# Mixers' out-projection: six of eight products as three fp32r products of split parts, the first of them moved into the recurrence's last chunk

## The reference, cut to what matters

```python
# per layer (twice); h is the normed, modulated input, 256 x 1024
o_att  = sliding_window_sink_attention(...)   # 512 features: 4 blocks of 128
o_rwkv = recurrence, group norm, bonus, gate  # 256 features: 2 blocks
o_conv = short gated convolution              # 256 features: 2 blocks
x = x + gate * (concat(o_att, o_rwkv, o_conv) @ w_mix_out)   # 1024 x 1024
x = x + gate2 * swiglu(norm(x))
```

## Time and profile before

| | before |
|---|---|
| median of 3 runs | 1794.88 us (1794.59 to 1794.94) |
| the profiled execution's own time | 1799.44 us |
| its span, first to last instruction | 1797.6 us |
| mean granted TensorE clock | 0.992 of full |
| layer 0: last output-projection product ends | 1052.84 us |
| layer 1: the same | 1601.94 us |

### The profile page before, as it was taken

How to read it: one execution, slowest core, us unless ns; L and a number is a source line. 1 busy time by engine, 2 the same in 40 slices (tenths; PEclk the granted TensorE clock), 3 DMA queues, 4 the chain that set the end, 5 groups by cost and what they waited for, 6 DMA issues and landing times.

```text
span 1797.6 us, 31559 instructions
## 1 busy us (share of the span) xinstructions
PE 1758.6 (98%) x13254; PEld 1604.7 (89%) x13254; DVE 1204.9 (67%) x1757; ACT 809.5 (45%) x1075; POOL 19.4 (1%) x25
## 2 busy tenths in 40 slices
PE   9999999999999999999999999999999999899999
PEld 8889879788887788999997799999999997789999
DVE  3895456777887877887637468777877456546443
ACT  2326443534576765434435254344443435335342
POOL 0000000000000000000000000000000000000000
PEclk9999999999999999999999899999999999999999
DMA  8434420787898986787441057876677432034442
GB/s 322 141 118 164 161 74 1 299 332 296 324 359 336 359 335 262 298 336 294 185 164 49 25 222 311 332 298 266 255 306 305 188 128 85 25 141 188 170 182 71
DMA packets 65228, 391.33 MB, mean 218 GB/s; under 512 B 7360, under 2 KB 7488, under 8 KB 27328
## 3 DMA queue, kind: packets, MB, share of 16 engines
q1 hardware_dynamic: 64800, 389.25, 56.0%
q10 hardware_dynamic: 288, 0.08, 0.0%
HBM read 388.25 MB, written 1.05 MB: 217 GB/s over the span
## 4 chain that ended last, share of the span: by engine, by line
PE 86%; DVE 8%; ACT 3%; issue 1%; DMA 1%; POOL 0%; SPq 0%; DVEq 0%; ACTq 0%
PE bank L526 85%; DVE region L2248 1%; PE bank L567 1%; DVE slab_low L1929 1%; ACT region L1432 1%; DMA slab<-in_w_up 0%; DVE region L1976 0%; DMA region<-in_w_down 0%; DVE tiny L1978 0%; DVE region L1987 0%; DVE region L2211 0%; DVE d_low L1936 0%; DVE tiny L2210 0%; DVE xT L2041 0%; DMA xT<-in_x 0%
## 5 line engine op out<-in xcount | busy, mean ns | idle before, releaser
L1929 DVE TENSOR_TENSOR slab_low<-slab,w_hi 128x2048 fp32r<-128x2048 f32 x152 | 346.5, 2292 | 94.3 <-ACT w_hi L1473 93.9
L526 PE MATMUL bank<-h_hi,w_hi 128*128 128x256 f32 x1408 | 391.7, 281 | 0.0
L526 PE MATMUL bank<-h_hi,slab_low 128*128 128x256 f32 x1408 | 390.9, 281 | 0.0
L526 PE MATMUL bank<-h_lo,w_hi 128*128 128x256 f32 x1408 | 380.2, 281 | 0.0
L1473 ACT ACTIVATE w_hi<-slab 128x2048 fp32r<-128x2048 f32 x152 | 291.1, 1917 | 86.9 <-DMA slab<-in_w_ffn_in 66.0
L526 PEld LDWEIGHTS bank<-h_hi,slab_low 128*128 128x128 f32 x1408 | 269.5, 191 | 0.0
L526 PEld LDWEIGHTS bank<-h_hi,w_hi 128*128 128x128 f32 x1408 | 264.7, 188 | 0.5
L526 PEld LDWEIGHTS bank<-h_lo,w_hi 128*128 128x128 f32 x1408 | 257.6, 188 | 0.0
L526 PE MATMUL bank<-gT_hi,d_hi 128*128 128x256 f32 x832 | 234.0, 281 | 0.8 <-DVE gT_lo L2126 0.8
L526 PE MATMUL bank<-gT_lo,d_hi 128*128 128x256 f32 x832 | 233.7, 281 | 0.0
L526 PE MATMUL bank<-gT_hi,d_low 128*128 128x256 f32 x832 | 233.6, 281 | 0.0
(11 more groups left out here) (282 smaller groups left out, 2856.2 us busy)
## 6 DMA issues: line engine op xcount, KB each, us to landing
slab<-in_w_ffn_in SPq DMA_DIRECT2D x88, 1024.0 KB, 8.4
slab<-in_w_up SPq DMA_DIRECT2D x64, 1024.0 KB, 8.7
region<-in_w_ada SPq DMA_DIRECT2D x128, 512.0 KB, 6.5
region<-in_w_ffn_out SPq DMA_DIRECT2D x44, 1024.0 KB, 4.8
region<-in_w_down SPq DMA_DIRECT2D x32, 1024.0 KB, 5.7
slab<-in_w_in SPq DMA_DIRECT2D x23, 1024.0 KB, 4.9
slab<-in_w_mix_in SPq DMA_DIRECT2D x20, 1024.0 KB, 8.2
hT<-in_w_ada SPq DMA_DIRECT2D x16, 512.0 KB, 7.6
```

The costliest lines, as they stand in the source:

```text
L526: return nc.tensor.matmul(o, lhsT, rhs, start=start, stop=True, skip_group_check=True)
L1929: V_.tensor_tensor(slab_low[slot][:, :], slab[slot][:, :], w_hi[h % 3][:, :].bitcast(F), ALU.subtract)\
```

## The change

The weights and the operands of j = 0 to 3 and 6, 7 are split; j = 4, 5 (the recurrence's part) stay plain. ACT makes the high part of out-slab c4 in chunk c4, in two pieces (1024 and 512 columns per partition), and of attention block c4 at the end of the chunk; DVE makes the low parts of slab c4 - 1 and attention block c4 - 1 at the start of chunk c4. The last attention block, the convolution and the last slab follow after the chunks. In chunk 3 TensorE does the products of j = 0 to 2 of block 0 ahead of its wait for `u_ready`, and those of block 1 ahead of the last attention output. The squares of the centred output move from `sq` to `V["kk"]`. In layer 0 SP's loads of w_ada (`ada_loads`, segment 2) now wait for the last out-slab to be used.

```diff
@@ the products (TensorE)
+                    def out_part(b, js):
+                        if b == len(places):
+                            if b % 2 == 0:
+                                out_slab()
+                            places.append(product("dve"))
+                        hi, lo, whole = slabs[b // 2]
+                        cols, ps = slice((b % 2) * P, (b % 2 + 1) * P), places[b][:, 0:T]
+                        for j in js:
+                            if j in (4, 5):
+                                m = mm(ps, whole[:, j, cols], V["yr"][:, j - 4, :])
+                                continue
+                            x_hi, x_lo = (o_hi[:, j, :], o_lo[:, j, :]) if j < 4 else \
+                                (cy_hi[:, j - 6, :], cy_lo[:, j - 6, :])
+                            mm(ps, hi[:, j if j < 4 else j - 2, cols], x_hi, j == 0)
+                            mm(ps, hi[:, j if j < 4 else j - 2, cols], x_lo)
+                            m = mm(ps, lo[:, j, cols], x_hi)
+                        return m
@@ in the chunks
                         outputs("vt", "C2T")
+                        if c4 == 3:
+                            pe.wait_ge(S["o_low"], w("o_low", 3))
+                            out_part(0, range(3))
                         pe.wait_ge(S["u_ready"], w("u_ready"))
...
                         m.then_inc(S["y_done" if c4 == 3 else "y_part"], 1)
+                        if c4 == 3:
+                            out_part(1, range(3))
@@ after the chunks
-                    pe.wait_ge(S["swa_ready"], w("swa_ready"))
-                    pe.wait_ge(S["conv_ready"], w("conv_ready"))
-                    out_early(0)
+                    pe.wait_ge(S["o_low"], w("o_low"))
+                    pe.wait_ge(S["cy_low"], w("cy_low"))
+                    out_part(0, (3, 6, 7))
                     pe.wait_ge(S["y_ready"], w("y_ready"))
                     mm(bank[7][:, :], C("half"), V["W"], True).then_inc(S["y_mean"], 1)
-                    out_early(1)
+                    out_part(1, (3, 6, 7))
                     pe.wait_ge(S["yc_sq"], w("yc_sq"))
-                    pair_sum(sq[:, 0:2, :])
+                    pair_sum(V["kk"])
                     for b in range(2, OUT_EARLY):
-                        out_early(b)
+                        out_part(b, (0, 1, 2, 3, 6, 7))
                     pe.wait_ge(S["mix_ready"], w("mix_ready"))
                     for b in range(KD):
+                        out_part(b, (4, 5) if b < OUT_EARLY else range(KD)).then_inc(S["for_dve"], 1)
@@ ACT, in each chunk
+                    slot, there = out_used[4 * l + c4]
+                    act.wait_ge(S[f"slab{slot}_in"], there)
+                    nc.scalar.activation(ow_hi[c4][:, 0:4 * T], slab[slot][:, 0:4 * T], ACT.Copy)\
+                        .then_inc(S["ow_high"], 1)
                     evac(short[4 + c4 // 2][:, (c4 % 2) * P:(c4 % 2 + 1) * P], P)
+                    nc.scalar.activation(ow_hi[c4][:, 4 * T:], slab[slot][:, 6 * T:], ACT.Copy)\
+                        .then_inc(S["ow_high"], 1)
...
+                    nc.scalar.activation(o_hi[:, c4, :], V["o"][:, c4, :], ACT.Copy).then_inc(S["o_high"], 1)
+                act.wait_ge(S["conv_ready"], w("conv_ready"))
+                nc.scalar.activation(cy_hi[:, :, :], V["cy"], ACT.Copy).then_inc(S["cy_high"], 1)
@@ DVE
                 for c4 in range(4):
+                    if c4:
+                        out_weights_low(c4 - 1)
+                        attended_low(c4 - 1)
                     ps = take()
...
                 dve.sem_inc(S["conv_ready"], 1)
+                attended_low(3)
+                dve.wait_ge(S["cy_high"], w("cy_high"))
+                V_.tensor_tensor(cy_lo[:, :, :], V["cy"], cy_hi[:, :, :].bitcast(F), ALU.subtract)\
+                    .then_inc(S["cy_low"], 1)
                 dve.wait_ge(S["y_done"], w("y_done"))
...
                 dve.sem_inc(S["yc_ready"], 1)
+                out_weights_low(3)
                 dve.wait_ge(S["rs"], w("rs"))
@@ SP
+                        if p == 0 and unit.seg == 2:
+                            name, k = slab_end[first_slab[unit.seg] - 1]
+                            sp.wait_ge(S[name], k)
```

More of the change, by code:

```diff
@@ L154 @@
     "conv_ready": "short convolution's output", "rho_done": "the state's part of a chunk's output",
+    "ow_high": "high part of a piece of output weights", "ow_low": "its low part", "o_high": "high part of attention",
+    "o_low": "its low part", "cy_high": "high part of the short convolution", "cy_low": "its low part",
     "y_part": "the output of a chunk",
@@ L423, in build @@
         B2["th"], B2["yr"] = B2["R"], B2["cs"]
+        ow_hi = [parts_at("ow_hi0", [6 * T], sq_at), over("ow_hi1", B2["pm"], (6 * T,)),
+                 parts_at("ow_hi2", [6 * T], silu_at), over("ow_hi3", m_hi_at_tt, (6 * T,))]
+        o_hi, o_lo = over("o_hi", m1_all, (4, T)), over("o_lo", B2["o"], (4, T))
+        cy_hi, cy_lo = over("cy_hi", B2["cc"], (2, T)), over("cy_lo", B2["cy"], (2, T))
         mix_hi = [over("mix_hi0", B2["AT"]), over("mix_hi1", B2["Tm"]), over("mix_hi2", B2["csp"])]
@@ L471, in build @@
         for_act, for_dve = [], []
-        low_used = []
+        low_used, out_used = [], []
         up_slab = []
@@ L1259, in short_half, with out_slab @@
                             used("for_act")
+                    slabs, places = [], []
+                    def out_slab():
+                        slot = n_slab[0] % SLOTS
+                        n_slab[0] += 1
+                        out_used.append((slot, w(f"slab{slot}_in", 16)))
+                        pe.wait_ge(S["ow_low"], w("ow_low", 2))
+                        n = len(slabs)
+                        slabs.append([v.rearrange("p (k c) -> p k c", c=T)
+                                      for v in (ow_hi[n][:, :], slab_low[slot][:, :], slab[slot][:, :])])
+                    def out_part(b, js):
[15 more added lines that the diff above has]
+                        return m
                     for c4 in range(T // CHUNK):
@@ L2611, in _ @@
             n_slab = [0]
+            first_slab = {}
             def before(n):
@@ L2652, in stream @@
                 for n, unit in enumerate(members):
+                    first_slab.setdefault(unit.seg, n_slab[0])
                     up_load(unit, source(unit, "up"))
```

34 lines of the change are left out of this document (13 added, 21 removed).

## The result

| | before | changed |
|---|---|---|
| median of 7 runs each | 1794.94 us (1794.59 to 1798.56) | 1803.4 us (1800.55 to 1805.85) |
| ratio of the times | | 1.004, 95% interval 1.0026 to 1.0054 |
| the profiled execution's own time | 1799.44 us | 1803.4 us |
| its span | 1797.6 us | 1801.6 us |
| mean granted TensorE clock | 0.992 | 0.994 |

A forecast was written before the change was run, and what follows sets the result against it. It took TensorE, busy 98% of the span, as the bound. Layer 0's -1.8, layer 1's -0.4 and a clock drop's +1.7 summed to -0.5 us, moved onto the median 1794.88: 1794.4 us, range 1790.9 to 1799.2.

The forecast's parts named there:

- The mechanism on which it rested most: Behind `mix_ready`: block 4 needs block 0's bank, waits for DVE's first residual, and TensorE stands still 3.4 us.
- Products: Out-projection: 48 of 64 products a layer become three fp32r products each, 4.0 us less TensorE time per layer.
- Low parts in the chunks: DVE's low parts ahead of the solutions: no cost in layer 0, chunk 3's solution 1.7 us late in layer 1.
- mean of layer 0: Start of the chain behind the last chunk: the mean can start at 1024.5 instead of 1025.93, 1.4 us earlier.
- From the mean to mix_ready: Chain from the mean to `mix_ready`: 7.6 us instead of 8.52, 0.9 less.
- standstill ahead of block 4: Out-projection behind block 3: TensorE idle 3.4 us, until DVE's first residual has read block 0's bank.
- `mix_ready` to the end: From `mix_ready` to the end of the out-projection: 18.9 us, where it was 18.4 before.
- The clock: TensorE's clock around the new idle times: one short drop in one of two layers, +1.7 us.
- sum of both layers: Whole kernel: -1.8 and -0.4 us for the layers, with the clock drop of 1.7 a sum of -0.5.
- the clock falls: Rival: clock falls behind block 3 in both layers, blocks 4 to 7 take 3.4 us longer each, 1799.5; chance 0.13.
- wait doesn't bite: Rival: DVE frees block 0's bank in time for block 4, 9.0 us saved, 1785.9 on the median's scale; chance 0.05.
- The low parts in chunks 1 and 2: Rival: they hold up the recurrence there too, +1.6 us, 1796.0; counted inside the forecast's 0.72. The forecast itself took 0.

The follow-up runs named there:

- e3_warm: Changed kernel with seven plain products on constants put in front of block 4, the bank wait kept: 1799.32 us, 1.0022 of the kernel before.
- after_again: The changed kernel, unaltered, timed and profiled once more: 1802.08 us, 1.0041 of the kernel before.
- e9_before_wait: Kernel before with three banks passed over ahead of block 4, so that it waits for block 0's bank: 1807.07 us, 1.0059 of the kernel before.
- e0_before: The kernel before, unaltered, timed and profiled once more: 1796.18 us, ratio 1.0004.
- e1_banks: Changed kernel whose blocks 4 and 5 pass over the banks of blocks 0 and 1: 1790.62 us, 0.9974 of the kernel before.
- e4_banks_low: e1_banks with DVE's low parts of the third and fourth weight slab made later: 1786.11 us, 0.9952 of the kernel before.
- e8_parts_only: e2_split_only with one plain product of the low parts in place of the three, output not the reference's: 1803.57 us, 1.005 of the kernel before.
- e2_split_only: Changed kernel without products in the last chunk, blocks 0 and 1 done whole behind it: 1795.07 us, 0.9997 of the kernel before.
- e6_fill_low: e4_banks_low with products of blocks 2 and 3 put ahead of the convolution's low part, block 4's ahead of `mix_ready`: 1787.59 us, 0.9955 of the kernel before.

## Why the prediction was wrong

It named 1794.4 us, no change that can be told (0.72), and a range up to 1799.2. It came out at 1803.4, slower. The mechanism on which it rested most was there; its prices were not.

| step, per layer unless said | predicted | measured |
|---|---|---|
| *Products*: TensorE's busy time | -4.0 | -8.1 in two layers |
| *Low parts in the chunks*, layer 0 / 1 | 0 / +1.7 | +1.6 / +1.6 (stage A) |
| mean of layer 0, in the profile | 1024.5 | 1024.14 |
| *From the mean to mix_ready* | 7.6 (-0.9) | 7.71 (-0.8) |
| standstill ahead of block 4 | 3.4 | 3.24 |
| `mix_ready` to the end | 18.9 | 19.3 without the fall (e3_warm), 20.9 with it |
| *The clock*, behind the standstill | +1.7 in one of two layers | +1.6 in both (profile), +1.3 in one of two (after_again) |
| sum of both layers | -0.5 | +7.4 (after_again) to +8.5 |

**The step that failed is *The clock*, with the baseline that goes with it.** It had two faults.

First, the count of the new falls. In the standstill the prediction took one fall in two layers, 1.7 in all. The profile shows one in each of its two layers, e9_before_wait one in each of its two, and after_again one in layer 0 and none in layer 1 (stage D 19.30). Its stretches, two around the standstills and one of stage B in layer 1:

```profile
1035.00:1041.00 6.00, 4.67 (x25) 4.59 (x26) 2.75 (x6) 2.83 (x3) 0.31 (x1) 0.72 0.98 407
1590.00:1596.00 6.00, 5.55 (x40) 5.38 (x41) 2.24 (x5) 2.96 (x3) 1.10 (x2) 1.00 1.02 429
1565.00:1574.00 9.00, 6.68 (x37) 5.58 (x37) 4.07 (x9) 1.81 (x4) 0.00 (x0) 0.50 0.07 31
```

e3_warm prices a fall at 1.6 in stage D, so 1.7 was the right size and the count was wrong. The rival *the clock falls* had the count right and 3.4 a layer as its price, twice too much; with everything else in it too low it named 1799.5, still 3.9 short. The Trainium skill's page TensorE: Matmul & The Clock Gate, section "HAM oscillation — how this bites in real kernels", describes a kernel in which TensorE waits about 3 to 5 us for DMA behind every short burst of products, and has the clock fall back in every one of these gaps. The standstills here are at the short end of that, 3.1 to 3.2 us, and five of the six looked at agree with it.

Second, the old falls. The execution on which everything was read had taken 4.6 us more than the median. (The 1.84 us that the section on the profile before calls outside the span lie outside it in every run, 1803.4 against 1801.6 in the table above; the 4.6 are all inside.) Stage A of layer 0 was 120.71 where e0_before has 117.66. Stage B held a lowered clock in both layers, and it does so in e0_before too; the changed kernel's profile has none there:

```profile
1021.00:1026.00 5.00, 4.77 (x13) 3.89 (x14) 0.31 (x1) 0.13 (x1) 0.00 (x0) 0.57 0.00 0
```

```profile
1018.00:1022.00 4.00, 4.00 (x13) 3.27 (x12) 0.15 (x1) 0.00 (x0) 0.00 (x0) 0.62 0.00 0
1564.00:1571.00 7.00, 6.38 (x21) 4.97 (x22) 1.76 (x4) 0.38 (x2) 0.00 (x0) 0.53 0.12 49
```

```profile
1018.00:1024.00 6.00, 3.84 (x37) 3.26 (x38) 3.97 (x8) 1.81 (x4) 0.00 (x0) 1.00 0.05 20
```

The first is the kernel before, layer 0 (layer 1 is in the earlier trace rows), the next two are e0_before, the last is the changed kernel. Against such stretches the prediction set a changed kernel "with the clock full throughout": it credited an early mean in layer 0 (-1.4), held the late solution of layer 1 paid for by the cheaper first block, and let a slow chunk hide the low parts (0). Against e0_before's layer 0 the changed kernel's A and B are 119.24 + 6.15 = 125.4, and 124.48 before: +0.9, not -1.4. Even that is too kind, since the 6.82 in it held a fall.

**The sum again, both kernels at full clock.** The kernel before would need about 5.1 us in B. This is an estimate from e0_before: 2.46 to block 0's first product (1015.01 to 1017.47), and the 2.6 that twelve records took at clock 1.00 behind the mean:

```profile
1022.69 2.75 PE L526 MATMUL bank<-region,slab 128*128 128x256 f32 x12
1025.28 1.02 PE L526 MATMUL bank<-sq,const 128*128 128x512 f32 x2
```

A +1.6, B +1.1 (6.15 against 5.1), C -0.8, D +0.85 (19.28 against 18.43): 2.7 a layer, 5.4 together, where the prediction had -2.2. The two falls behind the standstills add 3.2, which makes 8.6. Measured were 8.5, and 7.4 (5.0 to 9.7).

This leaves out the falls elsewhere, in the chunks and ahead of the mean (stage A 122.28 in both layers of the changed kernel's profile, B 9.20 in one layer of after_again). One could suspect that the added waits make them more frequent. The mean clocks of the timed runs speak against it. The changed kernel has 0.9927 over its 12 runs, the kernel before 0.9946 over 83, and e1_banks, whose chunks are those of the changed kernel, 0.9960 over 24. What the two falls behind the standstills cost, 3.2 us at half clock in place of full, lowers the mean by 3.2 of 1800, 0.0018, an estimate: that is nearly the whole 0.0019 by which the changed kernel lies below. So it lost about as much clock elsewhere as the kernel before did, in places that differ from one execution to the next. The prediction counted falls of the kernel before as saved, and as far as the mean clocks tell, the changed kernel kept as many.

**The rival *wait doesn't bite*** would have ended 9.0 us below the kernel before; e1_banks, in which the wait is gone, is 4.6 below (2.5 to 6.8). Its stage D gives 2.63 a layer, C gives 0.8 where the clock is full, A takes 1.6 back in both layers, which the prediction had charged in one, and B takes 1.1. **The low parts in chunks 1 and 2** held nothing up, as predicted: with chunk 3's moved away (e4_banks_low), stage A is that of the kernel before, 117.6.

Where the time went, each from the difference of two ratios, so that the rows add up to after_again's 7.4 by their making:

| step | us | give or take |
|---|---|---|
| making the parts (e8_parts_only) | +9.0 | 3.0 |
| three fp32r products for one plain one (e2_split_only) | -9.5 | 3.4 |
| the first products in the last chunk, no bank wait (e1_banks) | -4.1 | 2.7 |
| the bank wait that their place brings (after_again) | +12.0 | 3.2 |

The first three rows together, -4.6, are the gain that the change was able to have, and the last row more than takes it. With the bank chosen differently and two low parts moved (e4_banks_low), the same products bring 1786.11 us: 0.9952 of the kernel before (0.9939 to 0.9965), 8.6 us faster. It is the fastest of the kernels tried, though e6_fill_low (1787.59) cannot be told from it.

## What to carry to other kernels

When a product is moved earlier, it takes its buffer of a ring earlier as well: look who meets that buffer one turn later, and whether its reader stands behind other work. A standstill of the matrix engine can cost more than its length when dense work follows, here 5.1 for 3.2 in five of six cases, and each one has to be counted. Put both kernels at full clock before a saving is read off a place where the clock was low, and charge the new kernel the same falls as the old one until a run shows otherwise.

## What was not expected of the hardware

- One kernel's executions differ by where the clock falls. Two profiles of the kernel before differ by 4.2 us in their own time and by 4.0 in stages A and B of layer 0 alone (128.48 against 124.48), and the runs of the kernel before spread from 1789.84 to 1799.66 in one set.
- Products on constants, which compute nothing, made the kernel 3.4 us faster (give or take 3.2) by keeping the clock up over a wait of 3.2 us: 1.00 behind it, and stage D 1.6 shorter in each layer. The next real product came 0.22 us behind them in layer 0.
- The low part of 1024 columns and the 512 behind it took 1.83 us together on VectorE, so the slope between the 512 and 2048 columns of the kernel before (1.2 + 0.69) was right within 0.1.
